# The opening of a twelve-stage transformer kernel: first modulation weights in two pieces, strip units between them

## The reference

```
cond = jax.nn.silu(c)
mod = cond @ w_mod[l] + b_mod[l]
sh1, sc1, g1, sh2, sc2, g2, sh3, sc3, g3 = jnp.split(mod, 9, axis=-1)
h = modulate(x, norm_g[l, 0], sh1, sc1)          # rms_norm(x, g) * (1 + sc) + sh
x = x + 0.5 * g1[:, None, :] * swiglu(h, w_ffn1_gu[l], w_ffn1_down[l])
...
g, u = jnp.split(h @ w_gu, 2, axis=-1)           # swiglu
return (jax.nn.silu(g) * u) @ w_down
```

## Time and profile before

| | us |
|---|---|
| time, median of 3 runs | 1761.39 (1760.89 to 1761.67) |
| span of the profiled execution, first to last instruction | 1759.8 |
| TensorE busy | 1732.4 (98%) |
| VectorE busy | 1419.2 (81%) |
| ScalarE busy | 1006.7 (57%) |
| loads | 441.10 MB, 251 GB/s on average |

### The profile page before, as it was taken

The page is one execution under the profiler, slowest core; times in us unless marked ns, Lnnn a source line. Parts: engine busy times, 40 slices in busy tenths (PEclk is TensorE's granted clock), DMA queues, the critical chain, the costliest instruction groups (busy, mean ns, idle before and its releaser), DMA issues.

```text
span 1759.8 us, 24720 instructions
## 1 busy us (share of the span) xinstructions
PE 1732.4 (98%) x9178; PEld 1470.0 (84%) x9178; DVE 1419.2 (81%) x2185; ACT 1006.7 (57%) x1666; POOL 184.0 (10%) x382
## 2 busy tenths in 40 slices
PE   6999999999999999999999999999999999999998
PEld 3888888888888888988888888888888888888886
DVE  7899987898899888878888866579888876688565
ACT  5445577755475556877545644556455544465454
POOL 3021012111111111021110000001110000010000
PEclk9999999999999999999999999999999999999999
DMA  9999742699869985418898654459886483466551
GB/s 352 356 360 393 273 147 83 259 332 337 315 225 340 332 314 205 168 51 317 329 334 291 224 206 158 161 191 333 324 325 249 169 301 146 185 229 245 204 194 70
DMA packets 125144, 441.10 MB, mean 251 GB/s; under 512 B 15248, under 2 KB 18272, under 8 KB 124896
## 3 DMA queue, kind: packets, MB, share of 16 engines
q1 hardware_dynamic: 91024, 316.17, 49.1%
q0 software_dynamic: 33296, 120.12, 18.2%
q10 hardware_dynamic: 704, 3.23, 0.5%
HBM read 438.38 MB, written 1.09 MB: 250 GB/s over the span
## 4 chain that ended last, share of the span: by engine, by line
PE 94%; DVE 2%; DMA 2%; ACT 1%; issue 1%; SPq 0%; DVEq 0%; ACTq 0%
PE banks L2368 24%; PE banks L2169 15%; PE banks L2373 12%; PE banks L2147 11%; PE banks L2174 7%; PE banks L2152 6%; PE banks L2317 2%; PE banks L2321 2%; PE banks L2326 2%; PE banks L2137 1%; PE banks L2139 1%; PE banks L2138 1%; DMA weights_raw<-in_w_mod_first 1%; PE banks L2281 1%; DVE weights_lo L1355 1%
## 5 line engine op out<-in xcount | busy, mean ns | idle before, releaser
L1355 DVE TENSOR_TENSOR weights_lo<-weights_raw,weights_hi 128x1024 fp32r<-128x1024 f32 (+2 forms) x584 | 685.9, 1200 | 67.5 <-ACT weights_hi L810 66.7
L810 ACT ACTIVATE weights_hi<-weights_raw 128x1024 fp32r<-128x1024 f32 (+2 forms) x584 | 584.8, 1036 | 68.3 <-PE banks L2174 21.9
L2368 PE MATMUL banks<-hT,weights_hi 128*128 128x512 f32 x1856 | 464.1, 392 | 0.0
L2368 PEld LDWEIGHTS banks<-hT,weights_hi 128*128 128x128 f32 x1856 | 337.3, 189 | 63.0
L2373 PEld LDWEIGHTS banks<-hT,weights_lo 128*128 128x128 f32 x1856 | 253.2, 190 | 18.1
L1368 DVE CUSTOM_DVE_ANT_0 arena<-arena,mod_acc,vectors 128x1024 f32<-128x1024 f32 x216 | 267.6, 1280 | 0.0
L2373 PE MATMUL banks<-hT,weights_lo 128*128 128x256 f32 x1856 | 258.8, 282 | 0.0
L1004 ACT ACTIVATE arena<-banks 128x512 f32<-128x512 f32 x116 | 69.3, 598 | 323.1 <-PE banks L2373 322.9
L2147 PE MATMUL banks<-weights_hi,hT 128*128 128x512 f32 (+2 forms) x896 | 218.2, 385 | 0.0
L2147 PEld LDWEIGHTS banks<-weights_hi,hT 128*128 128x128 f32 x896 | 165.6, 188 | 29.9
L1690 DVE TENSOR_TENSOR arena<-banks,arena 128x512 f32<-128x512 f32 x116 | 79.8, 688 | 108.9 <-ACT arena L1004 108.9
(11 more groups left out here) (358 smaller groups left out, 1971.3 us busy)
## 6 DMA issues: line engine op xcount, KB each, us to landing
weights_raw<-in_w_ffn_gu SPq DMA_DIRECT2D x176, 512.0 KB, 4.5
arena<-in_w_mod POOLq DMA_DIRECT2D x128, 512.0 KB, 6.2
weights_raw<-in_w_in SPq DMA_DIRECT2D x104, 512.0 KB, 4.1
weights_raw<-in_w_ffn_down SPq DMA_DIRECT2D x88, 512.0 KB, 5.0
arena<-in_w_ada POOLq DMA_DIRECT2D x88, 512.0 KB, 5.6
weights_raw<-in_w_ffn_in SPq DMA_DIRECT2D x88, 512.0 KB, 4.1
weights_raw<-in_w_ffn_out SPq DMA_DIRECT2D x44, 512.0 KB, 4.5
weights_raw<-in_w_out SPq DMA_DIRECT2D x32, 512.0 KB, 3.8
```

Source lines behind the costliest of these rows:

```text
L810: nc.scalar.activation(whi[:, n % PARTS, 0:width], raw[:, slot, 0:width], ACT.Copy).then_inc(S("hi_done"), credit(n))
L1355: V.tensor_tensor(wlo[:, n % PARTS, 0:width], raw[:, n % RING, 0:width], whi[:, n % PARTS, 0:width].bitcast(F32), ALU.subtract).then_inc(S ...
L2368: T.matmul(half_banks(j)[:, kind, :], whi[:, n % PARTS, 256 * k + P * kind:256 * k + P * (kind + 1)], hx[:, :, 4 * q + k, :], start=q == 0 ...
```

## The change

The 16 modulation units are cut another way. A unit now holds, for one input block, 512 columns of scale and 512 of shift: units 0 to 7 (piece 0) give both vectors for column blocks 0 to 3, units 8 to 15 (piece 1) for blocks 4 to 7. `piece_store` takes a piece out and also makes its four scale columns. Weight units 6 and 7 are loaded behind modulation unit 9, units 8 and 9 behind 15, and strip 1 ahead of the constants. On TensorE `opening_high` (eight matmuls of a weight unit, four for each part of the input) and `opening_low` (the other four) take the place of `opening_strip`; those of the first two weight units stand between modulation units 10 to 15, the last two behind them, and the eight warm-up matmuls (`keep_warm`) are gone. ScalarE does all `scale_x` and `x_scaled` of groups 0 to 6, VectorE only group 7. The bias rounds are spread otherwise: `bias_take(3)` and `bias_reach(4)` behind the opening, `bias_reach(5)` behind `bias_take(4)`, `bias_pass(5)` behind the last unit of strip 1, each take in three reductions.

```diff
+MOD_PIECES = ((0, 8, 0, 4), (8, 8, 4, 4))
+PIECE_BANKS = (3, 4)
...
+            for m in range(0, 10):
                 mod_load(sp, m)
-            sp.wait_ge(S("mod_read"), 6)
-            gu_strip(RING, phases[0][2]["gu"], 0, (0,))
+            sp.wait_ge(S("mod_read"), reads_to(5))
+            first_weight(0)
+            first_weight(1)
+            for m in range(10, 16):
+                mod_load(sp, m)
             sp.wait_ge(S("mod_summed"), 1)
-            gu_strip(RING, phases[0][2]["gu"], 0, (1,))
+            first_weight(2)
+            first_weight(3)
             for kind, n0, a in phases:
                 if kind == "ffn":
                     if n0 == RING:
-                        sp.wait_ge(S("mod_summed"), 2)
+                        sp.wait_ge(S("mod_summed"), len(MOD_PIECES))
+                        gu_strip(n0 + 4, a["gu"], 1)
                         sp.dma_start(con[:, C_MASKW:], A["con"][:, C_MASKW:]).then_inc(S("const_loaded"), 16)
                         for dst, src in ((gq96[:, 0, :], "mla_q_norm"), (gq96[:, 1, :], "mla_k_norm"),
                                          (gw64[:, 0, :], "swa_q_norm"), (gw64[:, 1, :], "swa_k_norm"), (sink[:, :], "sinks")):
...
                 act.wait_ge(S("const_loaded"), 16)
                 nc.scalar.activation(table_col[:, :], ident[:, 0:1], ACT.Silu)
-                hi_static(RING, SLOT)
-                act.wait_ge(S("scale_ready"), 1)
-                act.wait_ge(S("mod_stored"), 2)
-                x_scaled(a, 0, True, (1,))
+                act.wait_ge(S("mod_stored"), 1)
+                x_scaled(a, 0, True)
                 x_hi(0)
                 x_scaled(a, 1, True)
                 x_hi(1)
-                act.wait_ge(S("mod_stored"), 3)
+                hi_static(RING, SLOT)
+                x_scaled(a, 2, True)
+                x_hi(2)
+                x_scaled(a, 3, True)
+                x_hi(3)
                 hi_static(RING + 1, SLOT)
-                x_hi(2)
-                x_hi(3)
-                hi_static(RING + 2, SLOT)
+                act.wait_ge(S("scale_ready"), 1)
                 x_scaled(a, 4, True)
                 x_hi(4)
-                hi_static(RING + 3, SLOT)
+                hi_static(RING + 2, SLOT)
+                x_scaled(a, 5, True)
                 x_hi(5)
                 x_scaled(a, 6, True)
                 x_hi(6)
-                x_scaled(a, 7, True)
+                hi_static(RING + 3, SLOT)
                 x_hi(7)
                 x_split_done()
             norm_stage(1, None)
...
+            def piece_store(i, a):
+                _, _, k0, blocks = MOD_PIECES[i]
+                dve.wait_ge(S("mod_summed"), i + 1)
+                eye = con[:, C_EYE:C_EYE + 32].unsqueeze(1).broadcast_to([P, 2 * blocks, 32])
+                sums = bank[PIECE_BANKS[i]][:, 0:64 * blocks].rearrange("p (k j) -> p k j", j=32)
+                cols = [w[:, 0:16].rearrange("p (c k) -> p c k", c=2)[:, :, k0:k0 + blocks] for w in (modc, vec)]
+                then(V.tensor_tensor(modm[:, 0:2 * blocks, :], sums, eye, ALU.mult))
+                then(V.tensor_reduce(modr[:, 0:2 * blocks], modm[:, 0:2 * blocks, :], AX, ALU.add))
+                then(V.tensor_tensor(cols[0], modr[:, 0:2 * blocks].rearrange("p (c k) -> p c k", c=2), cols[1], ALU.add))
+                last = i == len(MOD_PIECES) - 1
+                V.scalar_tensor_tensor(sclA[:, k0:k0 + blocks], modc[:, 8 + k0:8 + k0 + blocks], 1.0, vec[:, a["g"] + k0:a["g"] + k0 + blocks],
+                                       ALU.add, ALU.mult).then_inc(S("scale_ready" if last else "mod_stored"), 1)
...
             ins.then_inc(S("constants_set"), 1)
             bias_reach(0)
             bias_reach(1)
-            dve.wait_ge(S("const_loaded"), 16)
+            x_stats(1, 0)
             bias_take(0)
             bias_reach(2)
+            x_stats(1, 1)
             bias_take(1)
-            x_stats(1, 0)
-            x_scale0(1)
-            bias_reach(3)
-            bias_take(2)
-            x_stats(1, 1)
-            x_scale1(1)
-            mod_store(1)
-            scale_cols(phases[0][2])
-            bias_take(3)
-            bias_reach(4)
-            mod_store(0, 0, 2)
+            dve.wait_ge(S("const_loaded"), 16)
             phase = [0]
             ffn_n, mid1_n, mid2_n = [0], [0], [0]
             for kind, n0, a in phases:
                 phase[0] += 1
                 if phase[0] == 1:
-                    dve.wait_ge(S("mod_stored"), 2)
-                    x_scaled(a, 0, (0,), first=True)
-                    mod_store(0, 2, 8)
-                    dve.wait_ge(S("mod_stored"), 3)
+                    scales[0] += 1
+                    piece_store(0, a)
+                    bias_take(2)
                     x_low(0)
+                    x_low(1)
                     lo_static(n0, SLOT)
-                    x_scaled(a, 2, first=True)
-                    x_low(1)
-                    x_scaled(a, 3, first=True)
-                    lo_static(n0 + 1, SLOT)
                     x_low(2)
                     x_low(3)
+                    lo_static(n0 + 1, SLOT)
+                    bias_reach(3)
+                    piece_store(1, a)
+                    dve.wait_ge(S("scale_ready"), 1)
+                    x_low(4)
                     lo_static(n0 + 2, SLOT)
-                    x_low(4)
-                    x_scaled(a, 5, first=True)
-                    lo_static(n0 + 3, SLOT)
                     x_low(5)
+                    x_scaled(a, 7, first=True)
                     x_low(6)
                     x_low(7)
+                    lo_static(n0 + 3, SLOT)
                     x_split_done()
                 end = a["at"](UNITS_MID2) if kind == "mid2" else n0 + {"ffn": UNITS_FFN, "mid1": UNITS_MID1}[kind]
                 after = phases[phase[0]] if phase[0] < len(phases) else None
...
-                    units(n0 + 4, n0 + (8 if FIRST_TURNED[f] == 1 else 6))
                     if f == 0:
-                        bias_reach(5)
+                        units(n0 + 4, n0 + 5)
+                        bias_take(3)
+                        units(n0 + 5, n0 + 6)
+                        bias_reach(4)
+                    else:
+                        units(n0 + 4, n0 + (8 if FIRST_TURNED[f] == 1 else 6))
                     gated(0)
                     if f in loads_cond:
                         dve.wait_ge(S("cond_row_ready"), loads_cond.index(f) + 1)
                     for b in range(1, FIRST_TURNED[f]):
                         c = n0 + 4 + 6 * (b - 1)
-                        units(c + 2, c + 4)
-                        mod_units(mod_slot(f, b))
+                        units(c + 2, c + 3)
                         if f == 0 and b == 1:
                             bias_take(4)
+                            bias_reach(5)
+                        units(c + 3, c + 4)
+                        mod_units(mod_slot(f, b))
                         act_lo(b - 1)
                         units(c + 4, c + 6)
...
-                        if u == X_TURN_AFTER[0]:
-                            pe.wait_ge(S("const_loaded"), 16)
-                            x_turn(0, range(4), 1)
-                        if u == X_TURN_AFTER[1]:
-                            pe.wait_ge(S("bias_taken"), len(BIAS_AFTER))
-                            x_turn(1, range(4), 1)
-                    keep_warm(WARM[0])
-                    opening_strip(n0, strip_banks)
+                    mod_unit(0)
+                    mod_unit(1)
+                    mod_unit(2)
+                    bias_pass(0)
+                    mod_unit(3)
+                    mod_unit(4)
+                    bias_pass(1)
+                    mod_unit(5)
+                    mod_unit(6)
+                    pe.wait_ge(S("const_loaded"), 16)
+                    x_turn(0, (0, 1), 1)
+                    mod_unit(7)
+                    x_turn(1, (0, 1), 1)
+                    bias_pass(2)
+                    mod_unit(8)
+                    mod_unit(9)
+                    pe.wait_ge(S("bias_taken"), 3)
+                    x_turn(0, (2, 3), 1)
+                    x_turn(1, (2, 3), 1)
+                    pe.wait_ge(S("mod_stored"), 1)
+                    opening_high(n0, 0, hhi, "hhi_done")
+                    opening_high(n0, 0, hlo, "hlo_done")
+                    mod_unit(10)
+                    mod_unit(11)
+                    opening_low(n0, 0)
+                    opening_high(n0, 1, hhi, "hhi_done")
+                    opening_high(n0, 1, hlo, "hlo_done")
+                    mod_unit(12)
+                    mod_unit(13)
+                    opening_low(n0, 1)
+                    mod_unit(14)
+                    mod_unit(15)
+                    opening_high(n0, 2, hhi, "hhi_done")
+                    opening_high(n0, 2, hlo, "hlo_done")
+                    opening_low(n0, 2)
+                    bias_pass(3)
+                    opening_high(n0, 3, hhi, "hhi_done")
```

(6 more changed lines are left out.)

162 lines of the change are left out of this document (80 added, 82 removed).

## The result

The changed kernel takes 1765.69 us (median of 12 runs, 1764.47 to 1768.77), the kernel before 1761.66 beside it (12 runs, 1760.89 to 1763.03). The ratio is 1.0025, 95% interval 1.0016 to 1.0033: **4.0 us slower**. That is clear of zero. Whether it is over the 3.5 us (0.2%) which the prediction took as the edge of "the same" the interval leaves open; the median lies just beyond. The forecast was 1764.4, within 1760.6 to 1766.6. The time is inside the range, but more than one number on the way to it was wrong, and two of them cancelled.

The account below looks back on a forecast made before the run. TensorE's pace bounds the kernel from its first `down`, whose start weight unit 9's split, the condition row and VectorE's list set. 0.9 (opening) + 2.2 (reach) - 0.1 (takes) = +3.0 on 1761.39 gives 1764.4 us, range 1760.6 to 1766.6.

Parts of the forecast that it names:

- What bounds: From its first `down` at 58.48 the kernel runs at TensorE's pace; the change acts only through when that `down` starts.
- The converse claim: At strip 2's sums, 187.46, VectorE idles only 0.25 us; much more gained by TensorE alone would be lost there.
- VectorE's list, +2.1: From `gated(0)` to the last `bias_take`: `bias_reach(5)` adds 2.2 us, shorter takes save 0.1; 9.45 becomes 11.5.
- The opening, +0.9: Before strip 1: weight unit 9 is split on ScalarE at 40.15, 0.9 us later than in the kernel before.
- The condition row kept at 8.04: Load between weight unit 9's split and the gate's `Silu`: assumed to take 8.04 us as before.
- Rival 2: Constants delay the condition row's load between weight unit 9's split and the `Silu`; +4.2 us, 1765.6; chance 0.12.
- The warm-up matmuls at no cost: Opening: taking out the warm-up matmuls was listed as costing nothing, since TensorE was waiting there.
- rival 3's stall at 33.2: Opening: TensorE idles some 3.5 us at 33.2; any clock loss there was called covered, TensorE being early afterwards.
- Rival 3: Idle 2.7 us before the first `down` lowers TensorE's clock: at most +2.7, 1.4 taken; +4.4, 1765.8; chance 0.10.
- Rival 1: Before `gated(0)`: condition row lands 2 us or more sooner, VectorE's list alone sets the time; +0.9, 1762.3; chance 0.16.
- Rival 5: Opening loads: the two weights come late, queue dry 1 to 2 us, weight unit 9's split later; +4.5, 1765.9; chance 0.05.
- Rival 4: Faster: with VectorE no obstacle before the first `down`, it starts at 56.2; -2.3, 1759.1; chance 0.07.

Follow-up runs that it names:

- best_late_mod: best with one edit: GpSimd issues the six modulation loads four weight units later; 1759.76 us, ratio 0.9990.
- a_warm_all: Changed kernel plus multiplications by zero before the first opening matmuls, behind modulation unit 15 and before the first `down`; 1763.88 us, ratio 1.0011.
- a_reach5: Changed kernel with only `bias_reach(5)` moved back ahead of `gated(0)`; 1763.27 us, ratio 1.0009.
- b_reach5_late: Kernel before with only `bias_reach(5)` moved behind `bias_take(4)` and `bias_pass(5)` behind strip 1's last unit; 1764.98 us, ratio 1.0015.
- a_warm_down: Changed kernel plus twenty multiplications by zero in TensorE's idle time before the first `down`; 1764.42 us, ratio 1.0017.
- a_cond: Changed kernel with the condition row issued behind weight unit 7's split instead of unit 9's; 1765.13 us, ratio 1.0017.
- b_no_warm: Kernel before without its four multiplications by zero ahead of the opening; 1762.27 us, ratio 1.0001.
- best: Changed kernel with `bias_reach(4)`, `bias_reach(5)`, `bias_pass(5)`, `bias_take(5)` and the condition row earlier, plus the opening's multiplications by zero; 1764.02 us, ratio 1.0010.
- best_cold: best without the opening's multiplications by zero; 1762.23 us, ratio 1.0005.
- cold_late_mod: best_late_mod without the opening's multiplications by zero; 1761.32 us, ratio 0.9997.

## Why the prediction was right, and where it was wrong

*What bounds: right.* All is decided before strip 2, and what is lost there is lost at the end: 6.75 us at strip 2, 6.67 at TensorE's last matmul. It is not only the start of `down` that counts, though: of the 6.75 us, 3.89 are its later start, and 2.86 are `down` itself at the lower clock. The converse claim, that a gain much over 0.25 us would be lost to VectorE at 187, was wrong. best_late_mod has strip 2 earlier by 2.76 with no wait of TensorE up to 187, and keeps 2.2. One short pause in one place says that VectorE was waiting there (the row names ScalarE as what it waited for), not how much room it had.

*VectorE's list, +2.1: right in size.* Predicted 11.5 from `gated(0)` to the last `bias_take`; it is 11.5 in the changed kernel (50.76 to 62.27) and in a_warm_all (48.66 to 60.17). TensorE idle 2.56 for 2.7. That this list, with the clock that falls behind it, is most of the loss was shown from both sides: 2.6 of 4.0 us go with the reach (a_reach5), 3.2 come with it (b_reach5_late).

*The opening, +0.9: wrong in size.* Two errors against each other. With the clock up, weight unit 9 is split at 39.42 (a_warm_all), +0.16; I had modulation unit 15 read by 33.2, a step of estimates, and that comes sooner (31.51 + 1.07 = 32.6 in a_warm_all, 32.8 in a_warm_down). In the profiled execution, with the first opening matmuls at half speed, it is read at 34.4 and the split ends at 41.19, +1.9. a_warm_down, a_reach5 and a_cond have 39.5 to 39.7.

*The condition row kept at 8.04: right within half a microsecond.* 7.87, 7.66 and 7.54 in the changed kernel, a_reach5 and a_warm_all. Rival 2 is out: the constants are issued from 36.24 on, well ahead of the row, and it is not slower for them.

*The warm-up matmuls at no cost, and rival 3's stall at 33.2 "covered": this step failed.* I argued that TensorE was early afterwards. Before, its path had 0.3 us of slack; in b_no_warm's profile it is used up and `down` comes 0.9 us late, though the +0.5 of its times is within the noise. In the changed kernel, the opening's clock is worth 0.5 us of the median, against nothing in the ledger.

*Rival 3, the clock before the first `down`, 0.10: happened, in part of the executions.* I bounded it by 2.7, doubling 2.7 us of work; the profiled execution loses that (5.46 for 2.72) and a little more in the rest of `down`. Its price in the median, some 1.4, is my mid-value, and its time of 1765.8 came out nearer than the forecast's. One ground that I gave for it was weak: in the window from 8 to 9 us the profile of the kernel before puts the granted clock at 1.00, so the 1.08 us at 8.48 is slow without a lower clock on record. The price was right, but I gave it a chance of its own beside the forecast, as though a run either had it or not. It is a tax on a share of the executions, and belongs into the forecast: the ledger's true part is 2.1 (a_warm_all), the clock's 1.9, together 4.0. **The forecast of +3.0 was near in part by luck: an opening put too dear (0.9 for 0.16) stood in for some of a clock left out (1.9).** The prediction gave "the same" 0.56 and "slower" 0.37; the median lies just inside the second, and the interval reaches into both.

*Rival 1: the row as the gate is right, but the slack behind it thin.* Rival 5 did not come at its place: the queue does not run dry at 20 to 27 us. It does at 31 to 35 (67 GB/s, where before it moved 414), as strip 1's loads wait for the last modulation sums. I did not cost that, and no run prices it. Weight unit 14 comes at 55.87, where before ScalarE did not wait for it at 52.80. The rows give the larger part of that to its issue, at 43.19 instead of 40.83. It waits for VectorE's lower part of weight unit 9, and that came later: the unit was split at 41.19 for 39.26, and the change puts its lower part behind the rests of groups 6 and 7. From issue to use the load took 12.7 us, against 12.0 in b_reach5_late. In the changed kernel the reach hides the late load; in best, where the reach is mended, it became the bound.

*Rival 4: its sums and its chance disagree.* I put it at 1759.1, within 0.2%, and yet took nearly all of the 0.06 for "faster" from it.

## What to carry to other kernels

A step moved from in front of a wait to behind it cost its whole length here, and the idle time that it opened on TensorE could cost as much again through the clock: count it as part of the price, as a share of the executions. When one gate is taken away, look for those within a microsecond or two of it, and for who shares the queue with the load that becomes the next; a load issued earlier lets others start earlier too. And an opening that was tuned by small things (four multiplications by zero, a queue kept full) can lose them silently when its order is rewritten.

## What the runs showed of the chip

- The granted clock fell from 1.00 to 0.50 about TensorE's idle times, but not about each. At the first matmuls of the opening it fell with 1.59 us idle (the changed kernel, 23.68), and not with 1.39 to 1.65 (a_warm_down, a_reach5, a_cond, best_cold, cold_late_mod), where TensorE had done the same work. Ahead of `down` it fell with 2.56 us (the changed kernel) and 2.88 (a_cond), and not with 2.66 (b_reach5_late) or 1.63 (a_reach5). With the idle time of 3.63 us in the opening it fell in all six kernels that have it. So an idle time of 1.6 to 2.9 us made a fall possible here, and the execution decided. The Trainium skill, "TensorE: Matmul & The Clock Gate", "Part 1", says that the number of slow matmuls behind a start varies between runs of the same kernel; the rows agree.
- In the changed kernel's execution the clock stayed at 0.50 for some 3 us from about 24.2 on, half a microsecond after TensorE had started again, and for over 6 us from about 61.7 on, while it was still idle.
- Short multiplications by zero in three idle times held it at 1.00 in the profiled execution, and eleven runs then spread over 0.6 us, where twelve of the changed kernel spread over 4.3.
- Weight unit 14, 512 KB, took 12.0 to 14.3 us from its load's issue to its use with six 512 KB loads issued ahead of it in another queue (nine profiles in which ScalarE waited for it), 9.4 without (best_late_mod).
